# A new order of the opening of a block kernel: ACT's exponentials, sines and squares, DVE's reduction, and which engine issues which load

## The reference

```
u = rmsnorm(x) * g_mix;  z = u @ w_in                      # 512 x 1024
a = pool_mixer(z[:, :512])                                 # window means, small matmuls
s = ssm_mixer(z[:, 512:])                                  # 32 groups x 16 channels, 64 complex states, both directions
    dt = exp(log_dt); lam_bar = exp((a_re + i a_im) * dt)
    b_bar = (lam_bar - 1) / (a_re + i a_im) * B;  scan; C; gelu; gated linear unit
h = x + concat(a, s) @ w_out
h = h + hierarchical top-1 of 4 groups, top-2 of 8 experts (rmsnorm(h))
h = h + sigmoid(rmsnorm(h) @ ple_gate_w + b) * (p @ ple_proj_w)
out = rmsnorm(h)
```

## Time and profile before

| what | us |
|---|---|
| median of 3 runs | 521.2 (520.93 to 522.09) |
| profiled execution | 520.75 |
| its span | 518.7 |
| PE busy | 480.1 (93%) |
| DVE, ACT, POOL busy | 238.9, 159.8, 157.7 |
| mean granted clock of TensorE | 0.99 |

### The profile page before, as it was taken

How to read it: one execution, slowest core, us unless ns; L and a number is a source line. 1 busy time by engine, 2 the same in 40 slices (tenths; PEclk the granted TensorE clock), 3 DMA queues, 4 the chain that set the end, 5 groups by cost and what they waited for, 6 DMA issues and landing times.

```text
span 518.7 us, 7299 instructions
## 1 busy us (share of the span) xinstructions
PE 480.1 (93%) x2744; PEld 272.2 (52%) x2744; DVE 238.9 (46%) x685; ACT 159.8 (31%) x265; POOL 157.7 (30%) x140
## 2 busy tenths in 40 slices
PE   4899999999999999999999999779999988899993
PEld 3455776734854477765555555435454543444441
DVE  2799997999333257652222222111211211474525
ACT  6543434456442323121111111012211121213464
POOL 1069999954100001222222222202120210003250
PEclk9899999999999999999999999989999999999998
DMA  8874200399499975799999999999999997970012
GB/s 306 144 194 91 63 0 1 134 150 196 155 329 397 420 325 207 307 352 418 418 418 419 418 415 412 420 419 420 418 421 420 417 412 298 370 292 0 0 81 81
DMA packets 60091, 144.73 MB, mean 279 GB/s; under 512 B 27538, under 2 KB 36790, under 8 KB 47768
## 3 DMA queue, kind: packets, MB, share of 16 engines
q1 hardware_dynamic: 54456, 133.92, 70.1%
q0 software_dynamic: 5328, 10.31, 5.2%
q10 hardware_dynamic: 272, 0.04, 0.0%
HBM read 138.17 MB, written 14.19 MB: 294 GB/s over the span
## 4 chain that ended last, share of the span: by engine, by line
PE 65%; DMA 26%; ACT 3%; issue 3%; DVE 1%; SPq 1%; DVEq 0%; POOL 0%; POOLq 0%
PE bank L1597 60%; DMA big<-in_exp_w_up_dram 10%; DMA ring<-in_exp_w_up_dram 6%; DMA h<-in_exp_w_up_dram 6%; DMA moe<-v_d,gidx_all 4%; PE bank L1688 1%; DMA h<-in_x_dram 1%; PE bank L1948 1%; SPq L356 1%; ACT moe L537 1%; ACT L545 1%; PE bank L1832 1%; PE bank L2065 1%; PE bank L1967 1%; ACT moe L541 0%
## 5 line engine op out<-in xcount | busy, mean ns | idle before, releaser
L1597 PE MATMUL bank<-ring,moe 128*64 128x256 f32 (+3 forms) x976 | 127.4, 385 | 4.1 <-DMA ring<-in_exp_w_up_dram 3.6
L1597 PEld LDWEIGHTS bank<-ring,moe 128*64 128x64 f32 (+1 forms) x976 | 76.2, 144 | 38.5 <-issue 14.0
L1523 POOL DMA_INDIRECT pairs_d<-moe,sidx_all x32 | 31.9, 998 | 159.2 <-ACT moe L537 81.7
L862 DVE TENSOR_TENSOR vrow<-moe,bank 64x128 f32<-64x128 f32 x64 | 18.6, 291 | 122.2 <-ACT moe L761 121.2
L1597 PE MATMUL bank<-ut,big 128*128 128x512 f32 x128 | 59.0, 610 | 2.2 <-ACT ut L549 2.2
L1597 PE MATMUL bank<-big,ut 128*128 128x512 f32 x128 | 56.6, 595 | 1.2 <-ACT ut L682 1.2
L1597 PE MATMUL bank<-ring,ut 128*128 128x512 f32 x128 | 55.7, 593 | 0.2 <-DVE ut L862 0.2
L761 ACT ACTIVATE moe<-bank 64x256 f32<-64x256 f32 x32 | 12.1, 377 | 140.7 <-PE bank L1597 140.7
L537 ACT ACTIVATE moe<-bank 128x512 f32<-128x512 f32 x56 | 32.5, 598 | 60.1 <-PE bank L1597 49.5
L1597 PE MATMUL bank<-big,moe 128*64 128x256 f32 (+1 forms) x264 | 41.8, 427 | 6.7 <-DMA big<-in_exp_w_up_dram 4.0
L862 DVE TENSOR_TENSOR ring<-ring,bank 128x64 f32<-128x64 f32 (+1 forms) x142 | 39.5, 278 | 2.8
(11 more groups left out here) (193 smaller groups left out, 600.8 us busy)
## 6 DMA issues: line engine op xcount, KB each, us to landing
ring<-in_exp_w_up_dram SPq DMA_DIRECT2D x19, 1024.0 KB, 27.0
ring<-in_exp_w_down_dram SPq DMA_DIRECT2D x18, 1024.0 KB, 25.6
ring<-in_exp_w_gate_dram SPq DMA_DIRECT2D x17, 1024.0 KB, 21.5
big<-in_exp_w_gate_dram SPq DMA_DIRECT2D x7, 1024.0 KB, 17.0
big<-in_exp_w_down_dram SPq DMA_DIRECT2D x7, 1024.0 KB, 27.9
big<-in_exp_w_up_dram SPq DMA_DIRECT2D x6, 1024.0 KB, 18.7
ut<-in_exp_w_gate_dram SPq DMA_DIRECT2D x4, 1024.0 KB, 21.4
h<-in_exp_w_up_dram SPq DMA_DIRECT2D x4, 1024.0 KB, 24.7
```

The lines of the kernel that those rows point to most:

```text
L862: return dve.tensor_tensor(o, a, b, op)
L1523: pool.indirect_dma_start(pairs, bass.IndirectOffsetOnAxis(ap=index, axis=0), at(moe, ALL, M_Y + k * 512, [[1, 512]]), None, bounds_check= ...
L1597: return pe.matmul(o, a, b, start=start, stop=stop, skip_group_check=loose)
```

## The change

Seven edits, all in the opening:
- ACT issues g_mix last instead of first; log_dt comes first.
- ACT loads the Exp table first, waits for log_dt and a_re, and does the exponentials ahead of the first square. The Sqrt table is loaded between the first square and the first root. The sines come directly behind the Sin table and ahead of all takes. PE's wait ahead of its last block of the first tile is now for all four counts of `early` (exponentials and the g_mix copy).
- DVE does the angle reduction behind the first tile's normalising and ahead of the second's.
- SP loads only the identity (64 KB) between x1 and x2; the rest of the constants goes behind B and counts on `ld_poolw`, whose three waits become 9 loads.
- C and the six vector loads leave SP; POOL issues them after w_in's first part has landed.
- POOL casts `pair_i` ahead of the window means, after a wait for `ld_poolw`.
- POOL waits for no constants at its start.

```diff
--- before.py
+++ after.py
@@ -371,7 +371,7 @@
             for t in range(NT):
                 sp.dma_start(at(h, ALL, t * DM, [[1, DM]]), x_d[t * P:(t + 1) * P, :]).then_inc(ld_x[t], 16)
                 if t == 1:
-                    sp.dma_start(cst[:, :], A["consts"]).then_inc(ld_c, 16)
+                    sp.dma_start(ident, dr(A["consts"], C_ID, [[C_END, P], [1, P]])).then_inc(ld_c, 16)
             for j, done in ((0, ld_win0), (KC // 2, ld_winb)):
                 sp.dma_start(at(big, ALL, j * DP, [[DP, KC // 2], [1, DP]]),
                              dr(A["w_in"], DP + j * P * DM, [[DM, P], [P * DM, KC // 2], [1, DP]])).then_inc(done, 16)
@@ -380,17 +380,8 @@
                     sp.dma_start(at(ring, (d * NS, d * NS + NS), R_BRAW + n * G * CH, [[CH, G], [1, CH]]),
                                  dr(A[name], d * G * NS * CH, [[CH, NS], [NS * CH, G], [1, CH]])
                                  ).then_inc(ld_b, 16)
-            for n, name in enumerate(("ssm_c_re", "ssm_c_im")):
-                for d in range(2):
-                    sp.dma_start(at(ring, ALL, R_CRAW + n * 4 * P + d * NS, [[P, NB], [1, NS]]),
-                                 dr(A[name], d * G * CH * NS, [[NS, P], [GB * CH * NS, NB], [1, NS]])
-                                 ).then_inc(ld_craw, 16)
-            for n, name in enumerate(("pool_scale", "ssm_d", "glu_b")):
-                sp.dma_start(at(vrow, (4 * n, 4 * n + 4), 0, [[1, P]]),
-                             dr(A[name], 0, [[P, 4], [1, P]])).then_inc(ld_vec, 16)
-            sp.dma_start(at(vec, ALL, V_FFN, [[1, KC]]), dr(A["g_ffn"], 0, [[KC, P], [1, KC]])).then_inc(ld_vec, 16)
-            sp.dma_start(at(vrow, (12, 20), 0, [[1, P]]), dr(A["g_ple"], 0, [[P, KC], [1, P]])).then_inc(ld_vec, 16)
-            sp.dma_start(at(vrow, (20, 28), 0, [[1, P]]), dr(A["g_ffn"], 0, [[P, KC], [1, P]])).then_inc(ld_vec, 16)
+            sp.dma_start(at(cst, ALL, P, [[1, C_END - P]]),
+                         dr(A["consts"], P, [[C_END, P], [1, C_END - P]])).then_inc(ld_poolw, 16)
             sp.dma_start(at(big, ALL, KC * DP, [[DP, KC], [1, DP]]),
                          dr(A["w_in"], 0, [[DM, P], [P * DM, KC], [1, DP]])).then_inc(ld_win1, 16)
             sp.wait_ge(turned_ps, KC)
@@ -550,7 +541,6 @@
                                ).then_inc(ut_done, 1)
 
 
-            act.dma_start(at(vrow, (32, 32 + KC), 0, [[1, P]]), dr(A["g_mix"], 0, [[P, KC], [1, P]])).then_inc(ld_gain, 16)
             for d in range(2):
                 act.dma_start(at(ring, (0, G), R_LAM + 2 * P + d, [[1, 1]]),
                               dr(A["ssm_log_dt"], d * G, [[1, G], [1, 1]])).then_inc(ld_dt, 16)
@@ -558,8 +548,17 @@
                           dr(A["ssm_a_re"], 0, [[NS, G], [G * NS, 2], [1, NS]])).then_inc(ld_dt, 16)
             act.dma_start(at(ring, (0, G), R_LAM + P, [[NS, 2], [1, NS]]),
                           dr(A["ssm_a_im"], 0, [[NS, G], [G * NS, 2], [1, NS]])).then_inc(ld_small, 16)
+            act.dma_start(at(vrow, (32, 32 + KC), 0, [[1, P]]), dr(A["g_mix"], 0, [[P, KC], [1, P]])).then_inc(ld_gain, 16)
             act.wait_ge(eps_set, 1)
-            warm(0, ACT.Sqrt)
+            warm(0, ACT.Exp)
+            act.wait_ge(ld_dt, 48)
+            act.activation(at(ring, (0, G), R_LAM + 2 * P + 2, [[1, 2]]), at(ring, (0, G), R_LAM + 2 * P, [[1, 2]]),
+                           ACT.Exp).then_inc(early, 1)
+            act.wait_ge(early, 1)
+            for d in range(2):
+                act.activation(at(ring, (0, G), R_LAM + 4 * P + d * NS, [[1, NS]]),
+                               at(ring, (0, G), R_LAM + d * NS, [[1, NS]]), ACT.Exp,
+                               scale=at(ring, (0, G), R_LAM + 2 * P + 2 + d, [[1, 1]])).then_inc(early, 1)
 
             def x_squares(t):
 
@@ -574,28 +573,20 @@
 
             for t in range(NT):
                 x_squares(t)
+                if t == 0:
+                    warm(1, ACT.Sqrt)
                 x_root(t)
                 if t == 1:
                     act.wait_ge(c_ps, 1)
                     copy(at(vec, ALL, V_MIX, [[1, KC]]), at(bank[7], ALL, (NT - 1) * P, [[1, KC]]), early)
 
-            warm(1, ACT.Exp)
-            act.wait_ge(ld_dt, 48)
-            act.activation(at(ring, (0, G), R_LAM + 2 * P + 2, [[1, 2]]), at(ring, (0, G), R_LAM + 2 * P, [[1, 2]]),
-                           ACT.Exp).then_inc(early, 1)
-            act.wait_ge(early, 2)
-            for d in range(2):
-                act.activation(at(ring, (0, G), R_LAM + 4 * P + d * NS, [[1, NS]]),
-                               at(ring, (0, G), R_LAM + d * NS, [[1, NS]]), ACT.Exp,
-                               scale=at(ring, (0, G), R_LAM + 2 * P + 2 + d, [[1, 1]])).then_inc(early, 1)
             warm(2, ACT.Sin)
+            act.wait_ge(lam_red, 1)
+            act.activation(lam(8), lam(7), ACT.Sin).then_inc(lam_sin, 1)
+            act.activation(lam(9), lam(7), ACT.Sin, scale=0.5).then_inc(lam_sin, 1)
             for j in range(KC):
                 act.wait_ge(turned_ps, j + 1)
                 take(j, V_MIX)
-                if j == 2:
-                    act.wait_ge(lam_red, 1)
-                    act.activation(lam(8), lam(7), ACT.Sin).then_inc(lam_sin, 1)
-                    act.activation(lam(9), lam(7), ACT.Sin, scale=0.5).then_inc(lam_sin, 1)
 
             def zs_out(m):
 
@@ -887,15 +878,14 @@
             def lam3(k):
                 return at(ring, (0, G), R_LAM + k * P, gdn)
 
-            for t in range(NT):
+            def rows(t):
+
                 inverse(S_RS + t, 1, t + 1)
-                if t < NT - 1:
-                    normalise(moe, M_XN, t, S_RS).then_inc(xn_done, 1)
-            for first in (0, KC // 2):
-                normalise(moe, M_XN, NT - 1, S_RS, first, KC // 2).then_inc(xn_done, 1)
-
+                normalise(moe, M_XN, t, S_RS).then_inc(xn_done, 1)
+
+            rows(0)
             dve.wait_ge(ld_small, 16)
-            dve.wait_ge(early, 2)
+            dve.wait_ge(early, 1)
             seq(tt(lam3(5), lam3(1), dt, ALU.mult))
 
             seq(dve.tensor_scalar(lam(6), lam(5), 1.0 / TWO_PI, ROUND, ALU.mult, ALU.add))
@@ -905,6 +895,11 @@
             seq(dve.scalar_tensor_tensor(lam(5), lam(6), -TP3, lam(5), ALU.mult, ALU.add))
             dve.tensor_scalar(lam(7), lam(5), PI_LO, -PI_LO, ALU.min, ALU.max).then_inc(lam_red, 1)
 
+            for t in range(1, NT - 1):
+                rows(t)
+            inverse(S_RS + NT - 1, 1, NT)
+            for first in (0, KC // 2):
+                normalise(moe, M_XN, NT - 1, S_RS, first, KC // 2).then_inc(xn_done, 1)
             seq(tt(lam(10), are, are, ALU.mult))
             seq(tt(lam(11), aim, aim, ALU.mult))
             seq(tt(lam(10), lam(10), lam(11), ALU.add))
@@ -912,7 +907,7 @@
             dve.wait_ge(lam_sin, 2)
             seq(tt(lam(9), lam(9), lam(9), ALU.mult))
             seq(dve.tensor_scalar(lam(9), lam(9), -2.0, 1.0, ALU.mult, ALU.add))
-            dve.wait_ge(early, 4)
+            dve.wait_ge(early, 3)
             seq(tt(lam(12), lam(4), lam(9), ALU.mult))
             seq(tt(lam(13), lam(4), lam(8), ALU.mult))
             seq(dve.tensor_scalar(lam(5), lam(12), 1.0, None, ALU.subtract))
@@ -1101,7 +1096,7 @@
                 return dve.scalar_tensor_tensor(o, a, b, c, op0, op1)
 
             dve.wait_ge(wo0_done, 2 * NT)
-            dve.wait_ge(ld_poolw, 16 * 8)
+            dve.wait_ge(ld_poolw, 16 * 9)
             for n in range(4):
                 residual(n)
             norm(0)
@@ -1429,10 +1424,21 @@
             own.do(pool.memset(at(gidx_all, ALL, NE // 2, [[1, 1]]), 0))
             seq(pool.memset(fill[:, :], EMPTY))
             pool.dma_start(dr(tbl_d, 0, [[P, P], [1, P]]), fill[:, :]).then_inc(tbl_filled, 16)
-            pool.wait_ge(ld_c, 16)
-            own.do(pool.tensor_copy(pair_i[:, :], at(cst, ALL, C_PAIR, [[1, 2 * NT]])))
             for off in (0, PAD + T):
                 own.do(pool.memset(at(zbuf, ALL, Z_POOL + off, [[PW_, 4], [1, PAD]]), 0.0))
+
+            pool.wait_ge(ld_win0, 16)
+            for n, name in enumerate(("ssm_c_re", "ssm_c_im")):
+                for d in range(2):
+                    pool.dma_start(at(ring, ALL, R_CRAW + n * 4 * P + d * NS, [[P, NB], [1, NS]]),
+                                   dr(A[name], d * G * CH * NS, [[NS, P], [GB * CH * NS, NB], [1, NS]])
+                                   ).then_inc(ld_craw, 16)
+            for n, name in enumerate(("pool_scale", "ssm_d", "glu_b")):
+                pool.dma_start(at(vrow, (4 * n, 4 * n + 4), 0, [[1, P]]),
+                               dr(A[name], 0, [[P, 4], [1, P]])).then_inc(ld_vec, 16)
+            pool.dma_start(at(vec, ALL, V_FFN, [[1, KC]]), dr(A["g_ffn"], 0, [[KC, P], [1, KC]])).then_inc(ld_vec, 16)
+            pool.dma_start(at(vrow, (12, 20), 0, [[1, P]]), dr(A["g_ple"], 0, [[P, KC], [1, P]])).then_inc(ld_vec, 16)
```

(7 more changed lines are left out.)

## The result

The changed kernel took 524.09 us (median of 8 runs, 521.92 to 525.83), the kernel before 521.65 (median of 8, 520.70 to 524.40): a ratio of 1.0044 with a 95% interval of 1.0025 to 1.0063, 1.3 to 3.3 us slower. The forecast was 523.3, slower by 2.1. The profiled execution took 524.32, 3.57 above that of before; its span is 522.3.

What follows compares the result with a forecast made beforehand. It took PE (65% of the chain) and DMA (26%) as the bound; the fifth column block 2.1 us late on a profiled 520.75 gave 522.85, plus 0.45 to the median, 523.3 us. The 8-in-10 range was 520.9 to 526.0.

Steps and rivals of the forecast that it cites:

- W: Moment when ACT's early wait for the step sizes and a_re ends; taken as 7.8 us, bounds 4.9 to 8.85.
- ACT's sum, W + 10.2: ACT's exponentials, squares, roots, table loads and sines take 10.2 us from W, so the first take starts at 18.0.
- DVE and PE: Reduction delays the second tile to W + 7.6; PE's turning puts the first w_in matmul at W + 12.6, 20.4 us.
- The clock: No clock fall over PE's first ten matmul instructions: 4.3 us in place of 6.2, gain 1.85 us, bounds 0 and 1.85.
- The lambda tables: Last lambda product ready near 23.6 us, 1.1 before PE asks; no new wait, but the thinnest cover.
- POOL's loads: C and vector loads issued by POOL land at 21, 28 or 39 us by price; PE wants them at 27.9.
- Low to middle: Price cases taken for POOL's C loads: 0.56 to 2.3 us each, ten issues ending at 18.2 to 25.1, no wait.
- Passing on: A shift of the first w_in matmuls should reach the kernel's end nearly whole, as PE's progress releases loads and engines.
- early-loads rival: At ACT's first wait, small loads land before x crowds; fifth block 0.5 to 2.4 us early, 519.8; chance 0.13.
- late-POOL rival: C and vectors land late, say 33.4 us; PE stands 5.5 us at the first C block, 528.8; chance 0.12.
- clock rival: Turning's rate rises early and W is 7; first matmul 18.0, no change, 521.2; chance 0.15.

Runs made afterwards that it cites:

- small loads ahead of x: The changed kernel with SP issuing a_re and the second step size before x's first tile; ratio 0.9989 to the kernel before.
- the reduction last: The changed kernel with DVE's angle reduction back behind the last tile and the sines behind the third take; ratio 1.0043 to the kernel before.
- PE early in the changed kernel: The changed kernel with PE turning the identity 16 times ahead of the first tile; 522.06 us, ratio 1.0020 to the kernel before.
- the loads alone: The kernel before with only SP's and POOL's load part of the change, ACT and DVE orders as before; ratio 0.9982 to the kernel before.
- PE kept at work: The kernel before with PE turning the last block of the last tile 18 times more; ratio 1.0013 to the kernel before.
- the order alone: The changed kernel with all loads back where they were, g_mix still last on ACT's queue; ratio 1.0061 to the kernel before.
- The reduction first: As "small loads ahead of x", with DVE's angle reduction ahead of the first tile as well; 518.90 us against 521.14, ratio 0.9949.

## Why the prediction was right

The mechanism held: ACT's early wait for small loads, and the slow turning and the reduction behind it. The size of the opening's loss was forecast too large, 2.1 against 1.6 in the first pair of profiles and 1.3 over three. That the time came out within 0.8 us of the forecast (2.4 above the kernel before, forecast 2.1) is luck in part, since 1.1 of the 2.4 stand in no row of the opening. Step by step:

- **W, the end of ACT's first wait.** Put at 7.8, measured 7.56, 7.48 and 7.50. All of ACT's and DVE's work behind it starts from there: with it at 3.8 ("small loads ahead of x") the loss is gone. Within it one sub-step was wrong: I took the first step size to slip in ahead of x, as g_mix does. By 2.5 us ACT's queue had moved nothing in the changed kernel, where g_mix's load had moved 14 packets by 2.0 us in the kernel before; the only queue with packets was x's:

```profile
DMA packets 17, 0.07 MB, mean 28 GB/s; under 512 B 0, under 2 KB 0, under 8 KB 17
```

  The other error went the other way: I gave nothing for the constants out of the way, and they are worth 0.4 us of W (7.97 with them, 7.56 without). By the turns of whole packets (the Trainium skill, "DMA: Bandwidth & Descriptors", Queues, rings and completion order) I had estimated W near 7; the measured 7.5 lies between that and my value.
- **ACT's sum, W + 10.2.** The sines ended at 17.19, W + 9.6. Of the 0.6, 0.45 are the four tiles, 5.55 in place of 6.0: from a root to the next square it is 0.34 in the row that I took the earlier trace rows and 0.20 here (13.62 to 13.82). The row held a wait: the square at 6.33 stood until x's second tile landed at 6.3 (issued at 1.3, 5.0 us to landing), and behind W all of x is there. The exponentials and the copy were 0.09 shorter each, the sines 0.09 longer.
- **DVE and PE.** Second tile ready at W + 7.6: measured 15.12, W + 7.56. First matmul at W + 12.6: measured W + 12.2. The two parts are both real: without the reduction in between, the first matmul is 1.3 earlier ("the reduction last"), with quick turning 1.9 ("PE early in the changed kernel").
- **The clock.** No fall, ten matmul instructions in 4.53, forecast 4.3. But part of what this gives back would not have been usable before: PE would have waited for the tables, as the loads alone and PE kept at work show (0.98 and 0.97 us). So the fair comparison is of the tables' turning, 24.28 against 22.65, and there the forecast was 2.1 and the measured 1.63, or 1.34 over three profiles.
- **The lambda tables.** Forecast ready at 23.6, 1.1 ahead of PE; measured 22.70, 1.5 ahead. No new wait.
- **POOL's loads.** "Low to middle" was right: C at 0.8 each, vectors at 0.5 to 0.8, all issued by 19.6, and no wait at the C blocks. The rule of the Trainium skill ("SBUF — State Buffer", the box on DVE blocking DMA), that POOL can't write descriptors while DVE runs a fast-mode instruction, shows as a small thing here: the vector load issued at 16.27, beside the last normalising, took 0.79 where the same one took 0.56 with the loads alone. The other side shows as well: the normalising at 14.09 took 1.03 us in place of 0.75 while POOL was issuing, and with the order alone, where POOL issues nothing then, none took over 0.75. It held the second tile up by 0.28 us, which the sum had not. In the third profile of the changed kernel that tile took 0.75 and POOL's first pair of C loads 1.94 in place of 1.55, and the first matmul stood at 19.74 all the same.
- **Passing on.** The 1.62 at 24 us is 1.62 at 73.60 and still 1.62 at 204 us (PE's last logit matmuls end at 204.12 against 202.50). I had this as "nearly whole", and up to there it is. Behind 204 it is not shown: in the expert part the distance goes to 2.8, 4.5 and 3.6, by falls of the clock that come and go and by waits for weights. The reduction first is the best sign that a shift does pass: its stretch begins 2.7 us ahead of the mean of the kernel before, and its time is 2.7 below by the ratio (1.8 to 3.5).

The early-loads rival (0.13) failed at its first condition, the late-POOL rival (0.12) at its price, the clock rival (0.15) only in part: the clock did pay, but W was 7.5 and turning stayed slow for most of the blocks.

## What to carry to other kernels

An instruction that is moved ahead in an in-order queue takes its wait along, and what stood behind it inherits that wait: look up when its operands land, not how long it runs. The small loads here landed 3.3 to 6.9 us after their issues beside the big ones and 1.6 and 2.4 us after them where x was issued later; if anything waits for such a load early, issue it before them. Then move the work that hangs on it into idle time that exists, here DVE's first 8 us, and not between two steps of a pipeline. Done that way, the same idea that cost 0.4% gained 0.5%.

## What the runs showed of the hardware that was not expected

- A DMA of 512-byte rows issued first on ACT's queue at 0.87 had moved 14 of its 16 packets by 2.0 us, when x's queue had moved 7; a DMA of 4-byte elements issued at the same moment, 0.88, had moved none by 2.5, when x's queue had moved 17, and the step sizes landed 3.3 and 5.0 us after their issues. With the small loads ahead of x, the first step size, issued at 0.88 as well, landed in 1.6 us and a_im in 2.4.
- PE's idle time does not decide alone whether the granted clock falls: after 2.59 us of idle time it fell in one profile (the second of the kernel before) and did not in another (the loads alone), and after 1.94 it fell (the third of the kernel before).
- The column of the granted clock reads 1.00 from the start of the span, but the first blocks are turned at about half the rate of later ones (8 blocks in 1.97 us in the changed kernel's first tile, 24 in 2.84 with 16 turnings of the identity ahead; 32 in 6.24 with the reduction first, in 4.54 with 12 such turnings ahead).
- POOL issued a DMA of 512 runs of 256 bytes in 0.8 us, against 0.5 for one of 4 or 8 rows: the price hardly grows with the number of runs.
